# A ninth weight buffer in the two expert stages, and attention scores of neighbouring heads issued in pairs

## The reference, cut to what matters

```python
# first attention: 18 heads of 64 features in three groups of six, dilation 1, 4, 16
s = einsum('bdhnqe,bdhnke->bdhnqk', qs, kb) * 64**-0.5 + bias     # scores in windows
p = exp(s - s.max(-1)); o = einsum(p, vb) / p.sum(-1)             # softmax, values
# expert stage, once per layer l = 0, 1 (32 experts, top 2 of one group of 8)
h   = layer_norm(ALPHA * h + mixed, ln_g[l, 0], ln_b[l, 0])
hb  = silu(xb @ w_gate[e]) * (xb @ w_up[e]);  yb = hb @ w_down[e] # 1024x512, 1024x512, 512x1024
ffn = sum over the two experts of a token of gate * yb
h   = layer_norm(ALPHA * h + ffn, ln_g[l, 1], ln_b[l, 1])
```

## Time and profile before

| | us |
|---|---|
| runs (3): median, lowest, highest | 2379.5, 2378.51, 2381.85 |
| profiled execution, its own time | 2379.99 |
| its span | 2378.3 |
| PE busy / DVE / ACT / POOL | 2159.5 / 712.5 / 525.8 / 304.3 |
| line 1183 (expert gate and up), PE busy, both kinds | 412.4 + 151.1 |
| line 1196 (expert down), PE busy, both kinds | 211.9 + 87.5 |
| line 729 (dense projections), PE busy, 2000 records | 609.4 |

### The profile page before, as it was taken

How to read it: one execution, slowest core, us unless ns; L and a number is a source line. 1 busy time by engine, 2 the same in 40 slices (tenths; PEclk the granted TensorE clock), 3 DMA queues, 4 the chain that set the end, 5 groups by cost and what they waited for, 6 DMA issues and landing times. The chain is left out here.

```text
span 2378.3 us, 28492 instructions
## 1 busy us (share of the span) xinstructions
PE 2159.5 (91%) x11572; PEld 1235.2 (52%) x11572; DVE 712.5 (30%) x1558; ACT 525.8 (22%) x1219; POOL 304.3 (13%) x314
## 2 busy tenths in 40 slices
PE   7999989999999999879999999959997899999991
PEld 3446644444444578345555455547754555555550
DVE  1044235442664445362101111042125211110104
ACT  2123221022554144212121121130001212112111
POOL 0000000212232211101111111022000111111101
PEclk9999998999999999989999999979998899999996
DMA  9315243032003121238999999971233899999993
GB/s 346 134 36 183 72 154 123 29 150 71 1 1 110 71 72 49 63 157 336 426 423 423 423 423 423 416 281 42 83 115 138 335 424 421 425 423 423 423 412 123
DMA packets 100632, 545.90 MB, mean 230 GB/s; under 512 B 13360, under 2 KB 27481, under 8 KB 66554
## 3 DMA queue, kind: packets, MB, share of 16 engines
q1 hardware_dynamic: 79766, 495.65, 51.5%
q0 software_dynamic: 20384, 48.01, 5.6%
q10 hardware_dynamic: 340, 0.28, 0.0%
HBM read 538.79 MB, written 28.94 MB: 239 GB/s over the span
## 5 line engine op out<-in xcount | busy, mean ns | idle before, releaser
L729 PE MATMUL ps<-arena,ring 128*128 128x512 f32 (+11 forms) x2000 | 609.4, 464 | 10.6 <-DVE arena L2151 2.2
L729 PEld LDWEIGHTS ps<-arena,ring 128*128 128x128 f32 (+3 forms) x2000 | 359.1, 190 | 248.7 <-issue 205.4
L1183 PE MATMUL ps<-ring,arena 128*64 128x256 f32 x3648 | 412.4, 383 | 4.5 <-ACT arena L1605 3.2
L1183 PEld LDWEIGHTS ps<-ring,arena 128*64 128x64 f32 x3648 | 258.6, 138 | 137.8 <-ACT arena L1605 4.0
L810 PE MATMUL ps<-ring,arena 128*128 128x512 f32 (+1 forms) x560 | 249.4, 602 | 6.5 <-DVE arena L2142 4.2
L1196 PE MATMUL ps<-ring,arena 128*64 128x512 f32 x896 | 211.9, 617 | 21.6 <-DMA ring<-in_moe_w_down_dram 21.6
L2257 DVE SCALAR_TENSOR_TENSOR arena<-arena,ps 128x256 f32<-128x256 f32 x78 | 32.8, 421 | 562.8 <-ACT arena L1615 562.8
L2531 POOL DMA_INDIRECT assignment_rows<-arena x78 | 82.4, 1056 | 809.1 <-ACT arena L1621 780.9
L810 PEld LDWEIGHTS ps<-ring,arena 128*128 128x128 f32 (+1 forms) x560 | 102.5, 186 | 140.4 <-issue 140.1
L1183 PE MATMUL ps<-arena 128*64 128x256 f32 x1344 | 151.1, 380 | 0.0
L1196 PEld LDWEIGHTS ps<-ring,arena 128*64 128x64 f32 x896 | 66.0, 142 | 135.0 <-issue 103.1
(11 more groups left out here) (312 smaller groups left out, 1861.7 us busy)
## 6 DMA issues: line engine op xcount, KB each, us to landing
ring<-in_moe_w_gate_dram SPq DMA_DIRECT2D x48, 2048.0 KB, 22.9
ring<-in_moe_w_up_dram SPq DMA_DIRECT2D x48, 2048.0 KB, 26.2
ring<-in_moe_w_down_dram SPq DMA_DIRECT2D x48, 2048.0 KB, 21.4
arena<-in_moe_w_gate_dram SPq DMA_DIRECT2D x16, 2048.0 KB, 23.2
arena<-in_moe_w_up_dram SPq DMA_DIRECT2D x16, 2048.0 KB, 24.8
arena<-in_moe_w_down_dram SPq DMA_DIRECT2D x16, 2048.0 KB, 26.5
ring<-in_ada_w_dram SPq DMA_DIRECT2D x12, 2048.0 KB, 12.2
ring<-in_a_w_in_dram SPq DMA_DIRECT2D x12, 1536.0 KB, 14.7
```

The lines of the kernel that those rows point to most:

```text
L729: ins = pe.matmul(dst, w, m, start=i == 0, stop=i == len(pairs) - 1)
L1183: ins = pe.matmul(ps[CAP * i:CAP * (i + 1), bank_, 256 * j:256 * (j + 1)], rows_t[:, k, :], w[:, k, 256 * i:256 * (i + 1)], start=k == 0, ...
```

## The change

- `SLABS = 9`. The new slab 8 (`LENT`) covers words 4096 to 8191 of `arena`: the last tile of `X`, where `gate_b` now lives, and the lower part of `HT`. Slab 7 is words 8192 to 12287, slab 6 is at `R0 + 8576`. `arena` grows by the 1024 words of `gate_b`, which moves into it; the expert stage's working buffers move to `M0`.
- In layer 0 slab 8 is used up to expert position 24 (`LAST_LENT`). Then POOL loads the meta rows back from DRAM (`meta_back`), and DVE's `alpha(0, 4)` comes after block 34 in place of block 5.
- SP: seventh turn of a stage waits for what the eighth waited for and the other way round; the ninth, in slab 8, waits until all rows are in DRAM and the first gather has landed.
- `xe` has two buffers in place of three, so gathers run two pairs ahead.
- `load_lnp` of the stage's end moves: layer 0 from after block 10 to after the loads of `combined`; layer 1 to after the scatter of block 37.
- `scores_a` is called at even u alone and issues both units u and u+1: the same tile products of the two heads one behind the other, on partitions 0 to 63 and 64 to 127, into banks 4 and 5. It waits until unit u-1 has been read.

The diff, cut to its core (left out: the other addresses of `arena` that shift by 1024 or from `R0` to `M0`, an import, a blank line for an assertion, and a semaphore's declaration):

```diff
 RING = 6
-SLABS = 8
+SLABS = 9
 SLAB = 4096
+LENT = 8
+LAST_LENT = 24
...
         if kind == "expert":
-            i = n - TURN[("expert", l, (0, 0))]
-            cycle = [(ring_at + j) % RING for j in range(RING)] + list(range(RING, SLABS))
-            s = cycle[i % SLABS]
+            if n == TURN[("expert", l, (0, 0))]:
+                cycle = deque([(ring_at + j) % RING for j in range(RING)] + list(range(RING, SLABS)))
+            if cycle[0] == LENT and l == 0 and at_[0] > LAST_LENT:
+                cycle.popleft()
+            s = cycle[0]
+            cycle.rotate(-1)
...
+LENT_BACK = sum(s <= LAST_LENT for s, _ in BLOCKS)
...
-        arena = sb("arena", [P, 24576])
+        arena = sb("arena", [P, 25600])
-        gate_b = sb("gate_b", [P, D])
+        gate_b = arena[:, 5120:6144]
...
-        HT = at(5120, DC * TM).rearrange("p (c t) -> p c t", t=TM)
-        R0 = 9344
+        HT = at(6144, DC * TM).rearrange("p (c t) -> p c t", t=TM)
+        R0 = 10368
+        M0 = R0 + 1920
...
-        xe = [at(R0 + D * i, D) for i in range(3)]
+        xe = [at(M0 + D * i, D) for i in range(2)]
...
-            return ring[:, s * SLAB:(s + 1) * SLAB] if s < RING else at((5120, R0 + 8192)[s - RING], SLAB)
+            return ring[:, s * SLAB:(s + 1) * SLAB] if s < RING else at((R0 + 8576, 8192, 4096)[s - RING], SLAB)
...
                     if turn == first + RING:
+                        sp.wait_ge(*((yT_ready, DC) if l == 0 else (comb_done, COMBINED[(3, 3)] + 1)))
+                    if turn == first + RING + 1:
                         done(sp, f"router{l}_3")
-                    if turn == first + RING + 1:
-                        sp.wait_ge(*((yT_ready, DC) if l == 0 else (comb_done, COMBINED[(3, 3)] + 1)))
+                    if turn == first + RING + 2:
+                        sp.wait_ge(h_out, 16 * (5 if l == 0 else 9))
+                        sp.wait_ge(xe_landed[NPR * l % 2], 16 * (NPR * l // 2 + 1))
...
                 if u >= 2:
-                    pe.wait_ge(scores_read, u - 1)
-                b = ps[:, 4 + u % 2, :]
-                lo, c = 64 * (h % 2), h // 2
-                q, k = q_g[g][lo:lo + 64, c, :], k_g[g][lo:lo + 64, c, :]
-                if g == 0:
-                    k0, k1 = max(0, n - 1), min(NT, n + 2)
-                    ins = pe.matmul(b[:, 0:P * (k1 - k0)], q[:, P * n:P * (n + 1)], k[:, P * k0:P * k1], start=True, stop=True)
-                else:
-                    for n in range(NT):
-                        t = slice(P * n, P * (n + 1))
-                        ins = pe.matmul(b[:, t], q[:, t], k[:, t], start=True, stop=True)
-                ins.then_inc(scores_ready, 1)
+                    pe.wait_ge(scores_read, u)
+                c = h // 2
+                for n in (n,) if g == 0 else range(NT):
+                    t = slice(P * n, P * (n + 1))
+                    k0, k1 = (max(0, n - 1), min(NT, n + 2)) if g == 0 else (n, n + 1)
+                    o = 0 if g == 0 else P * n
+                    for i in range(2):
+                        q, k = (x[g][64 * i:64 * i + 64, c, :] for x in (q_g, k_g))
+                        ins = pe.matmul(ps[:, 4 + i, o:o + P * (k1 - k0)], q[:, t], k[:, P * k0:P * k1], start=True, stop=True)
+                        if g == 0 or n == NT - 1:
+                            ins.then_inc(scores_ready, 1)
...
-                if u < NUA:
+                if u < NUA and u % 2 == 0:
                     scores_a(u)
...
-                    if 1 <= n < (6 if l == 0 else 5):
+                    if 1 <= n < 5:
                         alpha(l, n - 1)
+                    if l == 0 and n == LENT_BACK + 3:
+                        vec.wait_ge(meta_back, 16)
+                        alpha(0, 4)
...
-                if J >= 3:
-                    pool.wait_ge(xt_done, J - 2)
+                if J >= 2:
+                    pool.wait_ge(xt_done, J - 1)
...
-                for j in range(3):
+                for j in range(2):
                     gather(l, j)
                 pool.wait_ge(tok_ready, 4 * l + 4)
+                gather(l, 2)
                 gather(l, 3)
-                gather(l, 4)
                 for n in range(NBS):
                     scatter(l, n)
-                    if n % 2 and (n + 9) // 2 < NPR:
-                        gather(l, (n + 9) // 2)
-                    if n == 10:
-                        pool.wait_ge(alpha_done, 5 if l == 0 else 9)
-                        load_lnp(3 + 2 * l)
+                    if n % 2 and (n + 7) // 2 < NPR:
+                        gather(l, (n + 7) // 2)
+                    if l == 0 and n == LENT_BACK:
+                        pool.wait_ge(*consumed(max(t for t in range(len(STREAM)) if SLOT[t] == LENT and STREAM[t][1] == 0)))
+                        pool.dma_start(X[0:META, 4, :], h_d[0][S:TM, :]).then_inc(meta_back, 16)
+                    if l == 1 and n == NBS - 2:
+                        pool.wait_ge(alpha_done, 9)
+                        load_lnp(5)
...
+                if l == 0:
+                    pool.wait_ge(alpha_done, 5)
+                    load_lnp(3)
                 pool.wait_ge(lnp_in, 32 * (4 + 2 * l))
```

More of the change, by code:

```diff
@@ L9 @@
+from collections import deque
 from contextlib import ExitStack
@@ L143, in place_slabs @@
     slot, use, prev, last, ring_at = [], [], [], {}, 0
-    for n, (kind, l, _) in enumerate(STREAM):
+    for n, (kind, l, at_) in enumerate(STREAM):
         if kind == "expert":
-            i = n - TURN[("expert", l, (0, 0))]
-            cycle = [(ring_at + j) % RING for j in range(RING)] + list(range(RING, SLABS))
-            s = cycle[i % SLABS]
+            if n == TURN[("expert", l, (0, 0))]:
[4 more added lines that the diff above has]
+            cycle.rotate(-1)
         else:
@@ L299, in build @@
         spec = sb("spec", [P, 64])
[L300 removed]
+        expert_of = arena[:, 25552:25584]
         group_of = sb("group_of", [P, NE])
         negm = sb("negm", [P, GROUPS, NT, HPG])
[L303 removed]
+        den = arena[:, 25472:25472 + GROUPS * NT * HPG].rearrange("p (g t h) -> p g t h", g=GROUPS, t=NT)
         nmax = sb("nmax", [P, 8])
         dsum = sb("dsum", [P, 8])
[L306 to L309, removed]
+        slot_tok = arena[:, 24784:24784 + NBLK].bitcast(I32)
+        half_id = arena[:, 24848:24848 + NBLK].bitcast(I32)
+        pair_tok = arena[:, 24904:24904 + NPR].bitcast(I32)
+        row_cols = arena[:, 24924:24924 + 4 * DC].rearrange("p (l i c) -> p l i c", l=2, i=2)
         key_bias = sb("key_bias", [P, NE])
@@ L372, in build @@
         cgs = [at(R0 + 5280 + 528 * i, NC_) for i in range(2)]
-        xe = [at(R0 + D * i, D) for i in range(3)]
[L375 to L379, removed]
+        xe = [at(M0 + D * i, D) for i in range(2)]
+        xeT = [at(M0 + 2048 + 1024 * i, 1024).rearrange("p (c t) -> p c t", t=P) for i in range(2)]
+        zg = [at(M0 + 4096 + 256 * i, 256) for i in range(2)]
+        hs = [at(M0 + 4608 + 256 * i, 256) for i in range(2)]
+        hb = [at(M0 + 5120 + 256 * i, 256).rearrange("p (c h t) -> p h c t", c=2, h=2) for i in range(2)]
+        yo = [at(M0 + 5632 + 512 * i, 512) for i in range(2)]
         yin = [at(R0 + 2 * D * i, 2 * D).rearrange("p (k d) -> p k d", k=2) for i in range(5)]
[L382 to L385, removed]
+        rw = at(R0 + 12672, 2 * DC * 36).rearrange("p (l c n) -> p l c n", l=2, c=DC)
+        rb = at(R0 + 13248, 72).rearrange("p (l n) -> p l n", l=2)
+        lg = at(R0 + 13320, 5 * 40).rearrange("p (t n) -> p t n", n=40)
+        RT = M0 + 4224
         elm = at(RT, 5 * NE).rearrange("p (t n) -> p t n", n=NE)
@@ L396, in build @@
         cnt = at(RT + 1120, 4 * NE).rearrange("p (n e) -> p n e", e=NE)
[L397 to L409, removed]
-        block_hot = at(R0 + 1856, 10 * NBLK).rearrange("p (i b) -> p i b", b=NBLK)
-        ovt = at(R0 + 6656, NOVER * NE)[0:1].rearrange("p (j e) -> p j e", e=NE)
+        key, key_col, heavy, base_of, need, over_at = (at(24960 + NE * i, NE) for i in range(6))
+        need_i = at(24960 + NE * 6, NE).bitcast(I32)
+        full = at(25184, NE)
+        above = at(25184 + NE, NE // 2).bitcast(BF16)
+        slot_i = at(25184 + 2 * NE, 10).bitcast(I32)
+        place_i = at(25184 + 3 * NE, 20).bitcast(I32)
+        rank = at(25184 + 4 * NE, NE)
+        slot_of = at(M0 + 20, 10).rearrange("p (t k) -> p t k", k=2)
+        place = at(M0, 10 * 2)
+        picked = at(M0 + 32, 2 * 5 * NE).rearrange("p (k t n) -> p k t n", k=2, n=NE)
+        emptied = at(M0 + 6400, NBLK)
+        row_hot = at(M0 + 576, 10 * P).rearrange("p (i r) -> p i r", r=P)
+        block_hot = at(M0 + 1856, 10 * NBLK).rearrange("p (i b) -> p i b", b=NBLK)
+        ovt = at(M0 + 5632, NOVER * NE)[0:1].rearrange("p (j e) -> p j e", e=NE)
         column_no = at(R0 + 14976, P)
@@ L471, in build @@
         order_ready, above_ready = sem("order_ready"), sem("above_ready")
-        xe_landed = [sem(f"xe_landed{i}") for i in range(3)]
```

(1 more changed line is left out.)

12 lines of the change are left out of this document (6 added, 6 removed).

## The result

| | before | changed |
|---|---|---|
| median of the runs, us | 2380.49 | 2355.74 |
| lowest to highest (4 runs each) | 2378.51 to 2381.85 | 2354.84 to 2358.12 |
| ratio, 95% interval | | 0.9898, 0.9881 to 0.9915 |
| span of the profiled execution | 2378.3 | 2354.4 |

A forecast was written before the change was run, and what follows sets the result against it. Transfers were taken to bind the expert stages, PE the first attention. Stages -14.3 us and paired scores -10.5 made -24.8 from 2380.0, 2355.2, stated as 2355.0; forecast 2350 to 2359 (0.62), range 2349 to 2364 (0.8).

The forecast's parts named there:

- Ninth slab: Expert stages: one more weight slab loads in the head's idle DMA time and stays ahead, -4.96 us in each stage.
- a stage that falls by under 5 us: Expert stages: a length falling by under 5 us would show the ninth slab step wrong, or PE the bound.
- Norm vectors: Expert stages: two 512 KB loads leave each stage's bound part, -2.48 us a stage, with +0.5 us at the last scatter.
- Meta reload: Expert stage of layer 0: reloading the meta rows moves 64 KB and costs 0.15 us.
- Two gather buffers: Expert stages: gathers issued three blocks ahead, some 33 us, land in 13.5 us at the longest, so no cost.
- rival 4: At `turn_pair`, 38 times after the heads: two gather buffers starve PE, each us of delay costing 38 us; 2393, chance 0.03.
- Paired scores: First attention: a pair's second score unit, on the other row half, is free; 13 pairs give 11.25 us, taken as -10.5.
- Rival 1: First attention: row halves overlap worse in most pairs, saving 8.3 or 4.4 us in place of 11.25; 2360.5, chance 0.14.
- Pairs that give nothing: First attention: pairs near 14 and 15, 22 to 25, and 30 and 31, where PE already waits, only wait longer.
- Tail: Layer 1's end: the last scatter may queue behind the moved norm vector loads, +0.5 us, bounds 0 and 2.5.
- Rivals 2 and 3: Head start misses the stages' ends, 2365, chance 0.10; the change does next to nothing, 2377, chance 0.05.
- rival 5: PE's late stage waits and slow products fall away, pairs shift transposes favourably: more gain than counted, 2346, chance 0.06.

The follow-up runs named there:

- four reloads: Changed kernel with layer 0's reload of the 16 meta rows issued four times, DVE waiting for all four; 2360.06 us, ratio 0.9914.
- Single scores: Changed kernel with the scores issued unit by unit as before, the rest of the change kept; 2369.86 us, ratio 0.9965.
- half by half: Changed kernel with the even head's four 4x128 tiles ahead of the odd head's four, not taking turns; 2363.92 us, ratio 0.9927.
- control: The changed kernel itself measured once more, nothing altered; 2357.58 us, ratio 0.9902 against the kernel before.
- no ninth slab: Changed kernel without the ninth slab in either layer, its two SP waits and the meta rows' reload; 2367.97 us, ratio 0.9949.
- given up in both: Changed kernel with slab 8 given up after position 24 in layer 1 too, without a reload there; 2359.09 us, ratio 0.9910.
- three buffers: Changed kernel with three gather buffers again in place of two, plus two small clears on DVE; 2354.89 us, ratio 0.9888.
- reload last: Changed kernel with three gather buffers, layer 0's meta rows reloaded after the last scatter but one, their `alpha` after the last block; 2356.36 us, ratio 0.9891.
- pairs alone: Kernel before with the paired scores added and nothing else of the change; 2368.67 us, ratio 0.9962.
- norm vectors back: Changed kernel with layer 1's two norm vector loads moved back to after block 10; 2362.06 us, ratio 0.9927.
- One row half: Changed kernel with both products of a pair on rows 0 to 63; 2368.74 us, ratio 0.9955.

## Why the prediction was right, step by step

*Ninth slab, -4.96 us a stage*: right in size. Without it, 3.9 and 5.9 us more, mean 4.9; in stage 0 the 3.9 are what is left after the reload's 0.7 us, so the slab alone is 4.6 there. The prediction named a stage that falls by under 5 us as a sign against this step. Stage 0 fell by 4.2, so the sign came, but it pointed at the wrong step: the loss sits in the gather buffers (1.6 to 2.1 us) and the reload (0.7). One reading was off as well: a slower product does not stand behind each wait; behind the 0.86 us of its own third row the product took the usual 3.65. "What it is ahead stays" when the slab is given up: shown by giving it up in both layers.

*Norm vectors, -2.48 us a stage*: right within what one execution can tell. Measured 2.1 in stage 1, and 0.4 back in the tail where I had 0.5. Between 120 and 200 us of stage 1, SP's queue moved 32.29 MB in the changed kernel and 31.18 with the vectors back, 1.1 MB, the whole of their bytes. The 0.8 MB of the expectation was the changed kernel against the one before, in which two buffers shift gathers into the same stretch. Layer 0 was not tried by itself.

*Meta reload, 0.15 us*: mis-sized, by taking bytes for the price. A further reload measured 0.7 us, and moving the only one out of the stage gave 0.5 (467.08 to 466.59). From 400 to 440 us of stage 0 the DMA moved 419 GB/s before, 416 in the changed kernel and 397 with four reloads, at shares of 1.00, 1.01 and 1.00: it does less work there at the same share.

*Two gather buffers, nothing*: this is the step that failed. I asked only if a gather would still arrive in time, and it did: PE never waited for one after a stage's head, so rival 4 is out. I did not ask where its bytes go. The fourth gather of each stage was in my own window of the idle head, and with two buffers it is not. Moving 0.5 MB from an idle stretch into a bound one costs 1.2 us at 423 GB/s; the buffer measured 1.6 to 2.1 us in stage 0 and about 0 to 0.7 in stage 1. That the buffer costs stage 0 is shown in both directions; that the moved bytes are the whole reason is argued from the queues. Why the stages differ is open: POOL issues the fourth gather 0.8 us ahead of the first gate product before, and 10 to 12 us behind it with two buffers, in both.

For stage 0 the account then agrees within the noise, with the prediction's slab and stage 1's vectors in it: -4.96 - 2.1 + 0.7 + 1.6 = -4.8 us against -4.2 measured, where kernels with the same stage code differ by up to 1.0 us. For stage 1: -4.96 - 2.1 and 0 to 0.7 give -7.1 to -6.4, against -7.0.

*Paired scores, -10.5 us*: right, -10.8 in the profiled execution, 6.0 to 12.4 by the runs. The clock has little part in it: between the first score and the first gate product PE's granted clock stood at 1.2 GHz for 70.7 us before and 69.6 in the changed kernel. Single scores, with 69.7 us, took 11.2 us longer than the changed kernel. That a pair costs one unit held in all three shapes, also at 16 records where only 4 were on record. The strict order of the Trainium skill ("TensorE: Matmul & The Clock Gate", What overlaps and what doesn't) is no objection: records may end in order and still lie beside each other. The same section of the Trainium skill lets a weight load pass running products only when the row group differs; with alternating halves that is always so, half by half only at the seam. The three times 1.16, 1.71 and 2.05 us run in that order, but no run here separates the load from the product. Rival 1 is out.

*Pairs that give nothing*: right for 30 and 31, where the wait grew from 5.74 to 6.81 us, for 14 and 15 (0.44 to 1.06) and near 22 to 25 (0.36 to 1.09).

*Tail*: +1.1 us against +0.5. The vectors explain 0.4. The kernels with the ninth slab also end 9.9 to 10.4 us after the last output's issue (2344.02 to 2354.4 in the changed kernel), those without it 9.5 to 9.7 (2368.70 to 2378.3 before). No run tells why.

*Ahead of the first score, -2.0 us*: no effect of the change. The control had it at 112.63, and the kernel before with two buffers, whose program is the same up to there, at 110.28. It made the profiled span look better than the sum deserved. Together with the 0.9 us between the stages, which no term had and no run explains, it hid the 3.1 us that stage 0 lacked. That they cancelled was luck; a right total was no proof of its terms.

Rivals 2 and 3 are out by the stages' 4.2 and 7.0 us, rival 5 by the time.

## What to carry to other kernels

When a buffer is taken from a prefetch, ask not only whether the transfer still lands in time, but in which stretch its bytes now move: out of an idle head into a transfer-bound body they cost 1.6 to 2.1 us in one stage here, for bytes worth 1.2, and at most 0.7 in the other. Two products that each use half the rows came at the price of one here when they alternated between the halves (16 records 1.16 us, as 8 do alone; half by half 1.71, on one half 2.05). Judge a change by stage, between two fixed instructions, since a right total can hide two terms that cancel.

## What the hardware showed that was not expected

A transfer of 16 rows of 4 KB cost the queue beside it 0.7 us where its bytes are 0.15 us (a third of what three more of them cost).

The granted clock falls to 1.2 GHz for about 3.4 us, behind short waits of PE (the first of 1.57 us at 112.55 in the changed kernel, the second of 1.06 us at 179.43), in some executions and not in others of the same instructions. Kernels with pairs come in two kinds: with a fall near 116 us and one near 185 us (no ninth slab, given up in both, three buffers, half by half, reload last), or with neither (the changed kernel, control, pairs alone, four reloads, norm vectors back). One row half, whose pairs are longer, has the first alone. What two such falls cost stands in the rows: the 14th pair starts 103.8 us after the first in every kernel with neither and 106.8 to 106.9 in those with both. Leaving half by half out, the first kind needs 955.5 to 957.9 us to stage 0, the second 952.8 to 954.9. There are more such places: the shortest of each kind, three buffers and four reloads, lack a fall near 580 us that the rest of both kinds have (half by half again left out). The stretch near 185 us (columns as in the earlier trace rows, clock third from last), reload last and then control:

```profile
185.00:188.40 3.40, 3.40 (x18) 2.10 (x19) 1.06 (x3) 0.54 (x2) 0.00 (x0) 0.53 0.02 5
```
```profile
182.50:186.00 3.50, 3.50 (x26) 2.77 (x27) 1.53 (x6) 1.50 (x5) 0.00 (x0) 1.00 0.02 5
```

PE is busy throughout in both. Single effects of 1 or 2 us in this kernel's total can thus be this and not the edit. So it is with *three buffers*: its two stages together are 2.8 us shorter than the changed kernel's, yet its profiled execution is 1.0 us longer, because the first score comes 2.5 us later and the way from there to stage 0 takes 1.0 us more. Its median is 0.9 us lower; where the clock fell in its other executions is not known.
